# A two-block transformer kernel: reciprocal spreads, band key, low halves and two gate tiles put in another order in the second block

## The reference, cut to what matters

```python
def rms_norm_2(x, g):
    xf = x.astype(jnp.float32)
    y = xf * lax.rsqrt(jnp.mean(xf * xf, axis=-1, keepdims=True) + EPS)
    return (y * g.astype(jnp.float32)).astype(x.dtype)

def mla_project(q_lat, kv_lat, g_qa, w_qb, g_kva, w_kvb):
    q = (rms_norm_2(q_lat, g_qa) @ w_qb).reshape(B, T, H_B, NOPE_B + ROPE_B)
    kv = (rms_norm_2(kv_lat, g_kva) @ w_kvb).reshape(B, T, H_B, NOPE_B + V_B)
...
def merge_branches(ya, yb, yc, za, zb, zc, ga, gb, gc, w_branch, w_o):
    m = (jax.nn.sigmoid(ga) * ((ya * jax.nn.silu(za)) @ w_branch[0])
         + jax.nn.sigmoid(gb) * ((yb * jax.nn.silu(zb)) @ w_branch[1])
         + jax.nn.sigmoid(gc) * ((yc * jax.nn.silu(zc)) @ w_branch[2]))
    return m @ w_o
```

## Time and profile before

| what | value |
|---|---|
| median of 3 runs | 3644.19 us (3641.17 to 3645.14) |
| span of the profiled execution | 3641.8 us |
| TensorE busy | 3507.4 us, 96% of the span |
| VectorE, ScalarE, GpSimd busy | 2077.0, 1483.7, 621.0 us |
| mean granted TensorE clock | 0.981 of 2.4 GHz |
| second block | from about 1925 us to the end |

### The profile page before, as it was taken

How to read it: one execution, slowest core, us unless ns; L and a number is a source line. 1 busy time by engine, 2 the same in 40 slices (tenths; PEclk the granted TensorE clock), 3 DMA queues, 4 the chain that set the end, 5 groups by cost and what they waited for, 6 DMA issues and landing times.

```text
span 3641.8 us, 54878 instructions
## 1 busy us (share of the span) xinstructions
PE 3507.4 (96%) x21361; PEld 3021.2 (83%) x21361; DVE 2077.0 (57%) x4352; ACT 1483.7 (41%) x2670; POOL 621.0 (17%) x549
## 2 busy tenths in 40 slices
PE   7999999999999998999998999999999879999997
PEld 5887887889999998999997568868888756777886
DVE  3253445679897558888885563293333346547443
ACT  3232333336667653333334552172212346436222
POOL 0000000006868754443330000000000000000000
PEclk9999999999999999999999999999999989999999
DMA  6224233479999999999992111101212211221232
GB/s 232 97 76 156 96 101 126 146 259 307 309 299 306 324 318 329 384 365 366 371 355 96 36 36 64 58 2 58 64 64 70 81 64 41 76 70 34 95 99 99
DMA packets 219744, 594.51 MB, mean 163 GB/s; under 512 B 17888, under 2 KB 101472, under 8 KB 216160
## 3 DMA queue, kind: packets, MB, share of 16 engines
q1 hardware_dynamic: 159312, 405.84, 32.3%
q0 software_dynamic: 36864, 134.23, 10.1%
q10 hardware_dynamic: 23312, 50.92, 3.7%
HBM read 530.11 MB, written 60.82 MB: 162 GB/s over the span
## 4 chain that ended last, share of the span: by engine, by line
PE 90%; DVE 4%; DMA 2%; ACT 2%; issue 1%; POOL 0%; ACTq 0%; DVEq 0%; SPq 0%
PE bank L796 65%; PE bank L1026 13%; PE bank L1150 3%; PE bank L993 2%; PE bank L1136 2%; PE bank L874 1%; PE bank L820 1%; DMA rows<-in_urows,rk 1%; DMA WR<-in_weights 1%; PE bank L907 0%; DMA gelu_by_expert<-geU 0%; DVE SrowA L2247 0%; PE bank L979 0%; DVE X L2395 0%; POOL rows L727 0%
## 5 line engine op out<-in xcount | busy, mean ns | idle before, releaser
L1676 DVE TENSOR_TENSOR WL<-WR,WH 128x1024 fp32r<-128x1024 f32 x512 | 628.1, 1229 | 773.6 <-ACT WH L1244 716.4
L1244 ACT ACTIVATE WH<-WR 128x1024 fp32r<-128x1024 f32 x512 | 537.0, 1057 | 703.8 <-PE bank L1026 299.2
L796 PE MATMUL bank<-H2h,WH 128*128 128x512 f32 (+1 forms) x1624 | 579.1, 357 | 4.5 <-DVE H2l L1704 4.5
L796 PE MATMUL bank<-H2h,WL 128*128 128x512 f32 (+1 forms) x1624 | 574.5, 354 | 0.0
L796 PE MATMUL bank<-H2l,WH 128*128 128x512 f32 (+1 forms) x1624 | 573.4, 353 | 0.0
L796 PE MATMUL bank<-Hh,WH 128*128 128x384 f32 (+1 forms) x1440 | 519.3, 361 | 0.3 <-DVE WL L1676 0.3
L796 PE MATMUL bank<-Hh,WL 128*128 128x384 f32 (+1 forms) x1440 | 505.9, 351 | 0.0
L796 PE MATMUL bank<-Hl,WH 128*128 128x384 f32 (+1 forms) x1440 | 505.6, 351 | 0.0
L1026 PE MATMUL bank<-ah,WH 128*128 128x384 f32 x1024 | 343.8, 336 | 14.7 <-issue 7.4
L796 PEld LDWEIGHTS bank<-H2h,WH 128*128 128x128 f32 x1624 | 307.8, 190 | 52.5 <-issue 7.7
L796 PEld LDWEIGHTS bank<-H2h,WL 128*128 128x128 f32 x1624 | 307.8, 190 | 43.2 <-issue 1.9
(11 more groups left out here) (361 smaller groups left out, 5588.9 us busy)
## 6 DMA issues: line engine op xcount, KB each, us to landing
WR<-in_weights SPq DMA_DIRECT2D x498, 512.0 KB
WR<-in_vrows SPq DMA_DIRECT2D x128, 512.0 KB
gelu_by_expert<-geU ACTq DMA_DIRECT2D x128, 192.0 KB
gates_by_expert<-tab SPq DMA_DIRECT2D x24, 1024.0 KB
geV<-gelu_by_expert SPq DMA_DIRECT2D x32, 768.0 KB
Gt<-gates_by_expert SPq DMA_DIRECT2D x14, 1536.0 KB
x_kept<-X ACTq DMA_DIRECT2D x2, 3072.0 KB, 10.4
X<-x_kept ACTq DMA_DIRECT2D x2, 3072.0 KB, 10.9
```

Of the source, the lines that this page charges most:

```text
L796: yield nc.tensor.matmul(b[0:rows, out_cols], a, r, start=n == 0, stop=n == len(pairs) - 1)
L1244: act.activation(WH[:, n % SLOTS, :, :].rearrange("p a b -> p (a b)"), WR[:, c % SLOTS, :, :].rearrange("p a b -> p (a b)"), ACT.Copy)\
L1676: v.tensor_tensor(WL[:, n % SLOTS, :, :].rearrange("p a b -> p (a b)"), WR[:, plan.splits[n] % SLOTS, :, :].rearrange("p a b -> p (a b)"), ...
```

## The change

Four places of the second block are put in another order, in both layers.

1. **Gate tiles.** Two of the four `z` tiles of branch 1 (`EARLY_Z`) are made in `queries_b`: tile 0 ahead of the sums of squares, tile 1 behind the spreads of the norms. ScalarE copies them raw into `yT` (`raw_z`) and applies Silu in place when the branch begins.
2. **Spreads.** With a second buffer `SG2`, in the place of `y2l`, all four spreads are issued at the branch's beginning.
3. **Band key.** `KEY_FIRST` makes the key the first tile of `queries_a`; every rotated tile raises `qk_ready`, attention A waits for the key and query 0 and then for one more query at a time, and VectorE's wait for the value copies stands behind the last addition.
4. **Low halves.** In `merge(2)` VectorE makes the low halves 0 to 3 ahead of the last merge step, and only 4 to 7 behind it.

```diff
 LOOK = 2
+EARLY_Z = 2
+KEY_FIRST = (4, 0, 1, 2, 3)
 MODS = (16, 24, 40, 48, 72, 96)
...
         def queries_a():
-            for f in range(6):
-                if f < 5:
+            for i in range(6):
+                if i < 5:
+                    f = KEY_FIRST[i]
                     p.chunk(("qa", l, f), ("qa", l, f))
                     both = upd or f == 4
                     p.job(("qa", l, f, "x"), "A", [] if both else [("qa", l, f)])
                     if both:
                         p.job(("qa", l, f, "c"), "A", [("qa", l, f)])
-                if f:
-                    p.job(("qap", l, f - 1), "V")
+                if i:
+                    p.job(("qap", l, KEY_FIRST[i - 1]), "V")
             p.chunk(("va", l), ("in2", l, IN_AT["va"]))
...
                 p.job(("hk", l, h, "c"), "A", [("hb", l, h)])
+        def z_tiles(b, f0, f1):
+            for f in range(f0, f1):
+                p.chunk((("z", b, l), f), (*(("za", l) if b == 0 else ("in2", l, IN_AT["zb"])), f))
+                for c in xc:
+                    p.job((("z", b, l), f, c), "A", [(("z", b, l), f)] if c == xc[-1] else [])
+
         def branch(b):
-            lin(("z", b, l), ("za", l) if b == 0 else ("in2", l, IN_AT["zb"]), "A", 4, xc)
+            z_tiles(b, EARLY_Z if b == 1 else 0, 4)
             if b < 2:
...
         def queries_b():
-            p.limit = len(p.splits) + QL + KVL
+            p.limit = len(p.splits) + QL + KVL + EARLY_Z
             for f in range(QL):
...
             p.job(("krb", l, "c"), "A", [("krb", l)])
+            z_tiles(1, 0, 1)
             p.job(("kvn", l), "A")
             p.job(("qn", l), "A")
             spreads(("kvn", l))
             spreads(("qn", l))
+            z_tiles(1, 1, 2)
             p.chunk(("vb", l), ("vb", l), False)
...
         y2h, y2l = place("y2h", B0 + 3072, 4, A, dt=f32r), place("y2l", B0 + 6144, 4, A, dt=f32r)
-        SG = place("SG", B0 + 19200, 2, A)
+        SG, SG2 = place("SG", B0 + 19200, 2, A), place("SG2", B0 + 6144, 2, A)
         C1, ZP = place("C1", B0 + 15360, 2, A), place("ZP", B0 + 16896, 2, A + 4)
...
             return SrowB[:, j, :] if j < 3 else PTB[:, :, :, :].rearrange("p a b c -> p a (b c)")[:, j - 3, :]
+
+        def spread_at(f):
+
+            return (SG, SG2)[f // 2][:, f % 2, :]
         def keys_of(h):
...
                     for s in range(n + 3):
-                        if kind == "A" and s == 0:
-                            pe.wait_ge(qk_ready, k.next(qk_ready))
+                        if kind == "A" and s < n and us[s][1] == 0 and us[s][0] < 4:
+                            pe.wait_ge(qk_ready, k.next(qk_ready, 1 if s else 2))
                         if kind == "B" and s < n and us[s][1] == 0:
...
                             fill(("Y", kind, l, u), calls)
-                def branch(b):
-                    for f in range(4):
+                def z_tiles(b, f0, f1):
+                    for f in range(f0, f1):
                         for c in xc:
                             linear((("z", b, l), f, c), (("z", b, l), f), H2, xcols(c))
+
+                def branch(b):
+                    z_tiles(b, EARLY_Z if b == 1 else 0, 4)
                     for f in range(4):
                         pe.wait_ge(inv_ready, k.next(inv_ready))
                         for c in xc:
                             def calls(bk, c=c, f=f):
                                 for n_, t in enumerate(range(0, TX) if c == "x" else range(TX, TA)):
-                                    yield nc.tensor.transpose(col(bk, n_), col(SG[:, f % 2, :], t),
+                                    yield nc.tensor.transpose(col(bk, n_), col(spread_at(f), t),
                                                               consts["ident"][:, :])
...
                     linear(("krb", l, c), ("krb", l), H2, xcols(c), P if c == "x" else QKB)
+                z_tiles(1, 0, 1)
                 sum_squares(("kvn", l), lambda j: lat_sq(QL + j), KVL, A)
                 sum_squares(("qn", l), lambda j: lat_sq(j), QL, A if upd else T)
                 spread_norm(("kvn", l), rk, A)
                 spread_norm(("qn", l), rt, A if upd else T)
+                z_tiles(1, 1, 2)
                 pe.wait_ge(lat_ready, k.next(lat_ready, KVL))
...
                                 .then_inc(p_ready, k.inc(p_ready))
+                def raw_z(f):
+                    for c in xc:
+                        out_of((("z", 1, l), f, c), yT[:, f, xcols(c)], slice(0, T if c == "x" else C))
+
                 def branch(b):
-                    for f in range(4):
+                    if b == 1:
+                        act.wait_ge(*k.own())
+                        for f in range(EARLY_Z):
+                            act.activation(yT[:, f, 0:w], yT[:, f, 0:w], ACT.Silu).then_inc(z_ready, k.inc(z_ready))
+                    for f in range(EARLY_Z if b == 1 else 0, 4):
                         for c in xc:
...
                     act.activation(lat_sq(j)[:, 0:wj], LAT[:, j, 0:wj], ACT.Square).then_inc(sq_ready, k.inc(sq_ready))
+                raw_z(0)
                 root(("kvn", l), rk, A, KVL * P)
                 root(("qn", l), rt, w, QL * P)
                 spread_norm(("kvn", l), rk, A)
                 spread_norm(("qn", l), rt, w)
+                raw_z(1)
                 act.wait_ge(x_kept, k.at(x_kept, 16 * (l + 1)))
...
                 def queries_a():
-                    for f in range(5):
+                    for i, f in enumerate(KEY_FIRST):
                         dst = qA[:, f, :] if f < 4 else kA[:, 0, :]
-                        tmp = SG[:, f % 2, 0:T]
+                        tmp = SG[:, i % 2, 0:T]
                         dve.wait_ge(act_read, act_at(("qa", l, f, "x")))
-                        v.tensor_tensor(dst[:, 0:T], R4[:, f % 3, :], cosA, ALU.mult)\
+                        v.tensor_tensor(dst[:, 0:T], R4[:, i % 3, :], cosA, ALU.mult)\
                             .then_inc(dve_step, k.inc(dve_step))
                         v.tensor_tensor(tmp, bank_of(("qap", l, f))[:, :], sinA, ALU.mult)\
                             .then_inc(dve_read, k.inc(dve_read))
                         dve.wait_ge(*k.own())
-                        if f == 4:
-
-                            dve.wait_ge(act_read, act_at(("vat", l, "c")))
-                        done = qk_ready if f == 4 else dve_step
-                        v.tensor_tensor(dst[:, 0:T], dst[:, 0:T], tmp, ALU.add).then_inc(done, k.inc(done))
+                        v.tensor_tensor(dst[:, 0:T], dst[:, 0:T], tmp, ALU.add).then_inc(qk_ready, k.inc(qk_ready))
+                    dve.wait_ge(act_read, act_at(("vat", l, "c")))
                 def project(h):
...
                     for f in range(8):
+                        if b == 2 and f == 7:
+                            for j in range(4):
+                                low_tile(H2l[:, j, 0:w], M4[:, j, 0:w], H2h[:, j, 0:w])
                         for c in xc:
...
                 def spread(f):
-                    v.tensor_copy(SG[:, f % 2, 0:w].rearrange("p (t s n) -> p t s n", s=2, n=64),
+                    v.tensor_copy(spread_at(f)[:, 0:w].rearrange("p (t s n) -> p t s n", s=2, n=64),
                                   inv[:, 0:w // P, 2 * f:2 * f + 2].unsqueeze(3).to_broadcast([P, w // P, 2, 64]))\
                         .then_inc(inv_ready, k.inc(inv_ready))
                 def branch(b):
                     dve.wait_ge(*k.own())
-                    spread(0)
-                    spread(1)
                     for f in range(4):
-                        dve.wait_ge(act_read, act_at((("z", b, l), f, xc[-1])))
+                        spread(f)
+                    for f in range(4):
+                        if b == 1 and f < EARLY_Z:
+                            dve.wait_ge(z_ready, k.next(z_ready))
+                        else:
+                            dve.wait_ge(act_read, act_at((("z", b, l), f, xc[-1])))
                         v.tensor_tensor(yT[:, f, 0:w], YT[:, f, 0:w], yT[:, f, 0:w], ALU.mult)\
...
                                             yT[:, f, xcols(c)], ALU.mult).then_inc(dve_read, k.inc(dve_read))
-                        if f + 2 < 4:
-                            spread(f + 2)
                     for f in range(4):
...
                 merge(2)
-                for f in range(8):
+                for f in range(4, 8):
                     low_tile(H2l[:, f, 0:w], M4[:, f, 0:w], H2h[:, f, 0:w])
```

More of the change, by code:

```diff
@@ L528, in build @@
         lat_ready = sem("lat_ready")
-        c_ready = sem("c_ready")
+        c_ready, z_ready = sem("c_ready"), sem("z_ready")
         block = ctx.enter_context(nc.Block())
@@ L1078, in queries_a @@
                                 linear(("qa", l, f, "c"), ("qa", l, f), H2, xcols("c"))
-                        if f:
-                            pe.wait_ge(act_read, k.reading(act_read, ("qa", l, f - 1, "x")))
```

(9 more changed lines are left out.)

3 lines of the change are left out of this document (removed).

## The result

The changed kernel takes 3617.47 us (median of 5 runs, 3613.2 to 3621.52), the kernel before 3644.19: ratio 0.9929, 95% interval 0.9917 to 0.9941. That is 26.7 us less; 24.4 were forecast. The profiled execution of the changed kernel spans 3611.5 us, 30.3 less than that of before.

A forecast was written before the change was run, and what follows sets the result against it. The prediction took TensorE, 90% of the chain that ended last, to bound the kernel. Its terms, 12 + 11 + 3 - 1.6 = 24.4 us, taken off 3644.2 gave 3620 us, with an 80% range of 3611 to 3631.

The forecast's parts named there:

- Term 1: Latent norms, both blocks: two gate tiles beside them fill TensorE's thin stretch, saving 12 us (bounds 7 and 14).
- A fall in one of the two blocks: Latent norms: TensorE's clock falls in one block; savings 6.7 or 4.6 us in block 0, 7.3 or 5.2 in block 1.
- the open stage: Latent norms: sums, root, reciprocal and spreads left uncovered between the two gate tiles, taken as 5.3 us in block 0.
- Term 2: Branch beginnings: four spreads issued together let transposes run back to back, saving 11 us (bounds 3 and 11.4).
- The tie forecast between gate tile and `y2l`: Branches of block 0: gate tile ends at 2217.0, low halves `y2l` at 2216.9, so it just fits.
- Term 3: Start of attention A: row maxima start where the key's addition stood, 1.48 us per block, 3 us (bounds 2 and 3.5).
- with the key done first: Start of attention A: with the key first, scores run while values are copied, saving 1.48 us per block.
- Term 4: Output projection: four low halves ahead of the last merge product lose 1.6 us (bounds +1 and -3.2).
- an earlier start may give that back: Projection in block 1: starting earlier may undo the 0.53 clock, so 1.0 us saved to 0.4 lost.
- the clock did not fall at every shortened gap: Rival, all four edited places: the clock falls at every shortened gap, leaving 17.6 us gained, 3626.6; chance 0.20.
- nor nowhere: Rival, all four edited places: the clock falls nowhere, giving 28.8 us gained, 3615.4; chance 0.15.
- VectorE's chain: Rival, branches: `y2l` replaces the spreads' wait; gains only 1.1 us per branch in block 0, 0.7 in block 1; chance 0.09.

The follow-up runs named there:

- experiment 7: Changed kernel with all low halves again behind the last merge product, and the projection's first two tiles making their high products first: 3606.85 us.
- experiment 4: Kernel before with only the two gate tiles moved beside the latent norms, the other three edits left out: 3627.25 us.
- experiment 5: Changed kernel with two more VectorE copies, into buffers nothing reads, ahead of the four low halves `y2l` of every branch 0 and 1: 3621.46 us.
- Experiments 3: Kernel before with only the four reciprocal spreads issued together, the other three edits left out: 3631.96 us.
- experiment 6: Changed kernel with the band key last again, but its addition not held behind the value copies; attention A waits for all five tiles: 3614.04 us.
- experiment 1: Changed kernel with all eight low halves behind the last merge product again: 3614.31 us.

## Why the prediction was right

**Term 1** was right in place and size: forecast 6.7 and 7.3 us with a full clock, measured 7.26 and 7.45, and 5.81 where the clock fell. "A fall in one of the two blocks" is what the changed kernel's profile shows, but not as a property of the code: of the seven profiles with this latent stretch, one shows the fall in block 1 and another one in block 0 (experiment 7, 5.69 gained). So it was luck that one fall was counted in and one came; with the clock held in both blocks the term is 14.7. What was off is the open stage, 4.54 us against 5.3.

**Term 2** was right for its reason: 2.60 against 2.65 in block 0, and in block 1 2.9 against 1.5 by the wait and 1.6 by the clock. In experiment 4 a branch of block 1 with the old order and a held clock gained 1.59, which leaves 1.3 for the wait. The tie forecast between gate tile and `y2l` came out at no wait in block 0 and 0.40 us in block 1 (forecast 0.5), and experiment 5 showed what stands behind it. Experiments 3 and 4 show that edits 1 and 2 work apart from each other.

**Term 3** was right in size in block 0 (1.43 against 1.48). Block 1 gave 1.92, and some 0.5 of it is the clock, which fell behind the wait for the key before and holds without that wait (experiment 4). The step behind the term was named only in part. The prediction said "with the key done first"; experiment 6 shows that the hold alone carried the cost.

**Term 4** was right in sign, and too small. For block 0 the loss was given as 1.1 us, or 2.8 with a fall of the clock; the pause was 3.29 us (forecast 3 to 4), the clock fell, and the loss was 1.89. In three profiles with this pause it was 1.89, 2.22 and 2.90. The step that failed is block 1's "an earlier start may give that back": TensorE paused twice there (0.82 and 1.90 us), the clock fell after the second pause, and the stage lost 0.64 us, outside the 1.0 saved to 0.4 lost. In experiments 5 and 6, with the same code, it held, and the stage gained 0.96 and 0.95. Against a kernel before whose clock holds there as well, edit 4 costs block 1 some 0.6 us (experiment 1).

The rivals: the clock did not fall at every shortened gap, nor nowhere. VectorE's chain took over as predicted in block 1, for 0.4 us, not the 2 us per branch of the rival. No term held the scatter ahead of the first edit, 11.7 us between single profiles, and the range left some 3 us beyond its cases; medians of five runs average part of it. That the total came within 2.3 us is therefore partly luck, as is that term 1 gave 1.1 us more and term 4 0.9 less than forecast, which nearly cancels. The ledger's 24.9 us against 24.4 is the firmer support.

## What to carry to other kernels

Fill a stage of norms with dense work whose operands are long ready, one piece per serial step. The gain can go beyond the listed waits: 7.3 us in block 0 with two tiles and 8.7 with three, where the listed waits for the latents were 3.8 us over both blocks. Where an operand comes in halves at different times, let TensorE run all products of the early half over several banks first, rather than making the late half earlier on an engine that has no idle time left from then on. Where noise is as large as the effect, compare leads of the same instruction at both ends of a stage; totals cannot tell 3 us from none here.

## What was not expected of the hardware

The same stretch of instructions, with TensorE busy 2.52 of 4.0 us, was followed by a granted clock of 0.53 in one execution and 1.00 in six others. At the projection the fall goes with the length of TensorE's wait, but not by a sharp line: behind 3.29 us it fell in three of three profiles (0.58, 0.50 and 0.71 over the next 4 us), behind 2.40 us in four of five, behind 2.13 or 2.15 us in three of six, behind 1.9 us in one of three, and behind 0.8 us in none. Behind the transposes of a branch it fell in four of eight branches with the old order (the kernel before and experiment 4), and in none of the 36 where the transposes run back to back. The Trainium skill, "TensorE: Matmul & The Clock Gate", section "HAM oscillation — how this bites in real kernels", has the work behind each pause of a thin matmul kernel start at half rate; the trace agrees for the pause of 3.29 us, and for the shorter ones and the thin stretches it is a matter of the single execution. What decides it there stays open: what differs from one execution to the next ahead of these stretches was not tried.
